# Chunk stage of a delta-rule mixer: two products of 128 columns with one stationary tile, and PSUM banks laid out anew

## What is computed

```python
def rwkv7_recurrence(r, decay, k, v, a, b):
    def step(state, inp):
        r_t, w_t, k_t, v_t, a_t, b_t = inp
        sa = jnp.einsum('bhij,bhj->bhi', state, a_t)
        state = (state * w_t[:, :, None, :]
                 + sa[..., None] * b_t[:, :, None, :]
                 + v_t[..., None] * k_t[:, :, None, :])
        y_t = jnp.einsum('bhij,bhj->bhi', state, r_t)
        return state, y_t
```

## Time and profile before

| | us |
|---|---|
| median of 3 runs | 2779.71 |
| lowest and highest | 2776.44, 2783.08 |
| profiled execution, its own time | 2776.74 |
| span of its trace | 2774.9 |
| TensorE busy in the span | 2632.4 |

### The profile page before, as it was taken

One profiled execution on the slowest core, in us unless ns is written; L12 is line 12 of the kernel. 1 busy time (PEld: TensorE's weight loads), 2 busy tenths in 40 slices (PEclk: granted clock), 3 DMA queues, 4 the chain that ended last, 5 costly groups with the idle time before them and its releaser, 6 DMA issues. The chain is left out here.

```text
span 2774.9 us, 55421 instructions
## 1 busy us (share of the span) xinstructions
PE 2632.4 (95%) x23093; PEld 2112.7 (76%) x23093; DVE 1573.4 (57%) x1945; ACT 1187.9 (43%) x1525; POOL 310.9 (11%) x356
## 2 busy tenths in 40 slices
PE   8999999999999988999999998998789999999998
PEld 7677778888777766888888887844678787788887
DVE  6747455244574655667766666467455555554462
ACT  5544343122464443555665554254224343432232
POOL 5022000000111401011111111021310000000002
PEclk9999999999999989999999999999999999999999
DMA  4200244333220022787778875312014252334341
GB/s 138 79 9 3 62 114 108 82 101 100 81 91 9 4 54 105 279 287 277 280 278 287 284 277 184 97 31 65 4 33 131 78 155 63 91 91 114 84 114 52
DMA packets 351896, 331.31 MB, mean 119 GB/s; under 512 B 17274, under 2 KB 269526, under 8 KB 351606
## 3 DMA queue, kind: packets, MB, share of 16 engines
q1 hardware_dynamic: 348101, 317.76, 36.9%
q0 software_dynamic: 3392, 11.14, 1.1%
q10 hardware_dynamic: 240, 0.07, 0.0%
HBM read 317.41 MB, written 11.53 MB: 119 GB/s over the span
## 5 line engine op out<-in xcount | busy, mean ns | idle before, releaser
L3109 DVE TENSOR_TENSOR experts_w_lo<-experts_raw,experts_w_hi 128x2048 fp32r<-128x2048 f32 (+1 forms) x81 | 167.8, 2079 | 77.3 <-ACT experts_w_hi L3065 75.7
L3109 DVE TENSOR_TENSOR experts_w_lo<-raw_in_act,experts_w_hi 128x2048 fp32r<-128x2048 f32 (+1 forms) x81 | 167.0, 2078 | 60.1 <-ACT experts_w_hi L3065 59.7
L3065 ACT ACTIVATE experts_w_hi<-raw_in_act 128x2048 fp32r<-128x2048 f32 (+1 forms) x81 | 139.7, 1745 | 50.8 <-DMA raw_in_act<-in_moe_up 45.2
L3278 PE MATMUL experts_psum<-experts_w_hi,experts_xg_lo 128*128 128x512 f32 x384 | 154.6, 403 | 5.5 <-DVE experts_w_lo L3109 4.3
L1555 PE MATMUL proj_psum<-keep_act_hi,proj_w_lo 128*128 128x512 f32 x360 | 152.2, 423 | 4.4 <-DVE proj_w_lo L1475 4.4
L3279 PE MATMUL experts_psum<-experts_w_lo,experts_xg_hi 128*128 128x512 f32 x384 | 150.4, 392 | 0.0
L3280 PE MATMUL experts_psum<-experts_w_hi,experts_xg_hi 128*128 128x512 f32 x384 | 150.2, 391 | 0.0
L3065 ACT ACTIVATE experts_w_hi<-experts_raw 128x2048 fp32r<-128x2048 f32 (+1 forms) x81 | 140.5, 1742 | 21.6 <-DMA experts_raw<-in_moe_gate 15.5
L1557 PE MATMUL proj_psum<-keep_act_hi,proj_w_hi 128*128 128x512 f32 x360 | 141.9, 394 | 0.0
L1556 PE MATMUL proj_psum<-keep_act_lo,proj_w_hi 128*128 128x512 f32 x360 | 141.5, 393 | 0.0
L831 PE MATMUL conv_ffn_psum<-keep_act_hi,conv_ffn_w_lo 128*128 128x512 f32 x336 | 132.0, 393 | 2.0 <-DVE conv_ffn_hid_lo L880 2.0
(11 more groups left out here) (896 smaller groups left out, 6807.9 us busy)
## 6 DMA issues: line engine op xcount, KB each, us to landing
raw_in_act<-in_moe_gate SPq DMA_DIRECT2D x33, 1024.0 KB, 8.5
experts_raw<-in_moe_up SPq DMA_DIRECT2D x32, 1024.0 KB, 10.5
experts_raw<-in_moe_down SPq DMA_DIRECT2D x32, 768.0 KB, 10.1
raw_in_act<-in_moe_down SPq DMA_DIRECT2D x32, 768.0 KB, 7.0
conv_ffn_raw<-in_w_ffn_in SPq DMA_DIRECT2D x43, 512.0 KB, 5.0
experts_raw<-in_moe_gate SPq DMA_DIRECT2D x17, 1024.0 KB, 9.0
raw_in_act<-in_moe_up SPq DMA_DIRECT2D x16, 1024.0 KB
proj_raw<-in_w_in SPq DMA_DIRECT2D x18, 768.0 KB, 4.4
```

The lines of the kernel that those rows point to most:

```text
L3065: act.activation(w_hi[v % 2][:, s], raw[ring][:, 0:n], ACT.Copy).then_inc(rounded, 1)
L3109: dve.tensor_tensor(w_lo[v % 2][:, s], raw[ring_of(2 * v + q)][:, 0:n], w_hi[v % 2][:, s].bitcast(F32), ALU.subtract).then_inc(split, 1)
L3278: pe.matmul(out, lhs[1][:, first + k, :], w_hi[slot][:, cols], start=begin and k == 0, stop=False)
```

## The change

1. A form takes 128 columns. `k` and `b` stay stationary, and one product now reads `q` and `a` side by side: an access of two rows of features apart (`r.qa_t`), 64 columns from each. Two forms of 16 products take the place of four. To have `q` and `a` at a fixed distance, `rw`, `bonus`, `g` and `kkb` become views of one tensor `all_rows`; `kkb` thereby lives through the two later parts of the mixer, which put `h_hi` and `o` into its place instead of allocating them.
2. The forms of a pair fill banks 0 to 3 wholly, 256 columns for each of the two results. VectorE masks in the order nt, qb, ak, qk.
3. The row halves of `nt` are exchanged by two products of 512 columns instead of 16 of 64, and wait for `z_kept`. Products with `v` are in the order z, y.
4. A result of a pair takes one bank (`one`, `at`) instead of half of two. In the levels, products use banks 0 to 3 in turn, squares banks 4 and 5 (for `x`) and 6 and 7 (for `xt`) in turn, so squares wait for the additions of two steps before instead of one.
5. `tz` takes banks 4 to 7, one a pair, and no longer waits for a copy.

```diff
-            return ps[:, 2 * s:2 * s + 2, 0:TT * CH].rearrange("p k (t n) -> p k t n", t=TT)
+        def raw(b, w):
+            return ps[:, b:b + 2, w * TT * CH:(w + 1) * TT * CH].rearrange("p k (t n) -> p k t n", t=TT)
+        def at_two(b, out, bank, t):
+            return ps[rows(out), b + bank, t * CH:(t + 1) * CH]
+        def one(b):
+            return ps[:, b, :].rearrange("p (k t n) -> p k t n", k=2, t=TT)
+        def at(b, out, k, t):
+            return ps[rows(out), b, (k * TT + t) * CH:(k * TT + t + 1) * CH]
...
-            def form(s, p, lhs, rhs, done):
+            def form(b, p, lhs, done):
                 for k, half, t in by_head:
-                    last = pe.matmul(place(s, half, k, t), lhs[rows(k), p, chunk(t, half)], rhs[rows(k), p, chunk(t, half)],
-                                     start=True, stop=True)
+                    both = ps[rows(half), b + k, :].rearrange("p (w t n) -> p w t n", w=2, t=TT)[:, :, t, :]
+                    last = pe.matmul(both, lhs[rows(k), p, chunk(t, half)], r.qa_t(rows(k), p, chunk(t, half)), start=True, stop=True)
...
             def swap_halves(p):
-                for k, half, t in by_chunk:
-                    last = pe.matmul(place(3, 1 - half, k, t), m.eye[rows(half), :], nt[rows(half), p, k, t, :], start=True, stop=True)
+                pe.wait_ge(z_kept, p + 1)
+                for half in range(2):
+                    last = pe.matmul(ps[rows(1 - half), 5, :], m.eye[rows(half), :], nt[rows(half), p].rearrange("p k t n -> p (k t n)"),
...
                 if p:
                     pe.wait_ge(formed, 4 * p)
-                if p >= 2:
-                    pe.wait_ge(x_new, p - 1)
-                    pe.wait_ge(z_kept, p - 1)
-                    pe.wait_ge(y_kept, p - 1)
-                    pe.wait_ge(nt_swapped, p - 1)
-                form(0, p, r.b_t, r.a_t, raw_n)
-                form(1, p, r.k_t, r.a_t, raw_a)
-                form(2, p, r.b_t, r.q_t, raw_q)
-                form(3, p, r.k_t, r.q_t, raw_k)
+                form(0, p, r.b_t, raw_b)
+                form(2, p, r.k_t, raw_k)
...
             def squares(l, p):
-                pe.wait_ge(p1_kept, from_1(l, p))
+                n = from_1(l, p) - 1
+                pe.wait_ge(p1_kept, n + 1)
                 pe.wait_ge(xt_new, step_of(l - 1, p))
-                if from_1(l, p) > 1:
-                    pe.wait_ge(xt_new, step_of(l, p) - 1)
+                if n >= 2:
+                    pe.wait_ge(xt_new, step_of(l, p) - 2)
                     if l < L - 1:
-                        pe.wait_ge(x_new, step_of(l, p) - 1)
+                        pe.wait_ge(x_new, step_of(l, p) - 2)
...
-            for s, done, dst, mask in ((0, raw_n, nt, m.before), (1, raw_a, ak, m.before), (2, raw_q, r.qb, m.upto),
-                                       (3, raw_k, qk, m.upto)):
+            for b, w, done, dst, mask in ((0, 1, raw_b, nt, m.before), (0, 0, raw_b, r.qb, m.upto), (2, 1, raw_k, ak, m.before),
+                                          (2, 0, raw_k, qk, m.upto)):
...
+                r.qa_t = lambda rows, p, cols: all_rows[rows, p:p + to_keys + 1:to_keys, cols]
```

More of the change, by code:

```diff
@@ L1103, in _ @@
             from_v(pairs - 1)
-            pe.wait_ge(nt_swapped, pairs - 1)
             swap_halves(pairs - 1)
             def products(l, p):
+                n = from_1(l, p) - 1
                 pe.wait_ge(masked, step_of(l, p))
                 pe.wait_ge(x_new, step_of(l - 1, p))
-                if l == 1:
-                    pe.wait_ge(x_new, pairs)
-                    pe.wait_ge(z_kept, pairs)
                 for k, half, t in by_chunk:
-                    last = pe.matmul(place(p % 2, half, k, t), nb[rows(1 - half), p, k, t, :], x[rows(1 - half), p, k, t, :], start=True,
+                    last = pe.matmul(at(n % 4, half, k, t), nb[rows(1 - half), p, k, t, :], x[rows(1 - half), p, k, t, :], start=True,
                                      stop=True)
@@ L1130, in squares @@
                     if l < L - 1:
-                        last_x = pe.matmul(place(2, 1 - half, k, t), xt[rows(half), p, k, t, :], p1[rows(half), p, k, t, :], start=True,
+                        last_x = pe.matmul(at(4 + n % 2, 1 - half, k, t), xt[rows(half), p, k, t, :], p1[rows(half), p, k, t, :], start=True,
                                            stop=True)
-                    last = pe.matmul(place(3, half, k, t), p1[rows(half), p, k, t, :], xt[rows(half), p, k, t, :], start=True, stop=True)
+                    last = pe.matmul(at(6 + n % 2, half, k, t), p1[rows(half), p, k, t, :], xt[rows(half), p, k, t, :], start=True, stop=True)
                 if l < L - 1:
@@ L1149, in _ @@
                 for k, half, t in by_half:
-                    last = pe.matmul(place(p % 2, k, half, t), r.a_tok[rows(half), t, cols(p, k)], xt[rows(half), p, k, t, :],
+                    last = pe.matmul(at_two(2 * (p % 2), k, half, t), r.a_tok[rows(half), t, cols(p, k)], xt[rows(half), p, k, t, :],
                                      start=True, stop=True)
                 last.then_inc(w_full, 1)
-                if p == 1:
+                if p == 2:
                     pe.wait_ge(xt_new, L * pairs)
-                if p >= 2:
-                    pe.wait_ge(tz_kept, p - 1)
                 pe.wait_ge(z_kept, p + 1)
                 for k, half, t in by_chunk:
-                    last = pe.matmul(place(2 + p % 2, half, k, t), xt[rows(half), p, k, t, :], z[rows(half), p, k, t, :],
+                    last = pe.matmul(at(4 + p, half, k, t), xt[rows(half), p, k, t, :], z[rows(half), p, k, t, :],
                                      start=True, stop=True)
@@ L1191, in first_level @@
                 dve.wait_ge(y_full, p + 1)
-                dve.tensor_tensor(x[:, p], eight(m.eye[:, :]), slot(0), ALU.add).then_inc(x_new, 1)
+                dve.tensor_tensor(x[:, p], eight(m.eye[:, :]), one(4), ALU.add).then_inc(x_new, 1)
             for p in range(pairs):
-                for s, done, dst, mask in ((0, raw_n, nt, m.before), (1, raw_a, ak, m.before), (2, raw_q, r.qb, m.upto),
-                                           (3, raw_k, qk, m.upto)):
+                for b, w, done, dst, mask in ((0, 1, raw_b, nt, m.before), (0, 0, raw_b, r.qb, m.upto), (2, 1, raw_k, ak, m.before),
+                                              (2, 0, raw_k, qk, m.upto)):
                     dve.wait_ge(done, p + 1)
-                    dve.tensor_tensor(dst[:, p], slot(s), eight(mask[:, :]), ALU.mult).then_inc(formed, 1)
+                    dve.tensor_tensor(dst[:, p], raw(b, w), eight(mask[:, :]), ALU.mult).then_inc(formed, 1)
                 if p:
@@ L1206, in _ @@
                         dve.wait_ge(x_new, step_of(l - 1, p))
-                        dve.tensor_tensor(x[:, p], x[:, p], slot(2), ALU.add).then_inc(x_new, 1)
+                        dve.tensor_tensor(x[:, p], x[:, p], one(4 + (from_1(l, p) - 1) % 2), ALU.add).then_inc(x_new, 1)
                     dve.wait_ge(xt_full, from_1(l, p))
                     dve.wait_ge(xt_new, step_of(l - 1, p))
-                    dve.tensor_tensor(xt[:, p], xt[:, p], slot(3), ALU.add).then_inc(xt_new, 1)
+                    dve.tensor_tensor(xt[:, p], xt[:, p], one(6 + (from_1(l, p) - 1) % 2), ALU.add).then_inc(xt_new, 1)
             for p in range(pairs):
@@ L1213, in _ @@
                 dve.tensor_copy(r.tz_tok[:, :, p * P:(p + 1) * P].rearrange("p t (k d) -> p k t d", k=2),
-                                slot(2 + p % 2)).then_inc(tz_kept, 1)
+                                one(4 + p)).then_inc(tz_kept, 1)
 def scan_and_read_phase(m, r, then):
@@ L4239, in rows_job, with cross_mixer @@
     return job
-def cross_mixer(m, q, k, mem_hi, mem_lo):
+def cross_mixer(m, q, k, mem_hi, mem_lo, o_at):
     i = m.ins
```

70 lines of the change are left out of this document (35 added, 35 removed).

## The result

The changed kernel takes 2771.54 us (median of 8 runs, 2759.22 to 2778.42), the kernel before 2784.45 beside it (8 runs, 2776.44 to 2793.46). The ratio is 0.9948, 95% interval 0.9928 to 0.9967: by the ratio 14.5 us less, by the two medians 12.9, against 13.2 forecast. The profiled execution spans 2776.6 us, 1.7 more than that of before. The stage itself gave 15.6 us back, so the windows come first: forms, levels 1 to 4, level 5 and the end, and the scan behind them (columns as in the earlier trace rows).

What follows compares the result with a forecast made beforehand. Code fetch for TensorE was taken as the floor, with waits for other engines added where pauses fall between. Savings of 8.2 + 2.9 + 2.1 = 13.2 us from the median of 2779.71 gave 2766.5 us, range 2759 to 2775.

Steps and rivals of the forecast that it cites:

- The bound: Whole stage: TensorE waits for its code, in blocks of some 126 load-and-matmul pairs, 3.75 us each.
- Forms and first level: Forms part: fewer, wider matmuls mean less code, 24.7 us against 32.88, 8.2 us less.
- the turn: Forms part, each pair after the first: forms, first level, z, y, exchange and wait for z, 5.7 us.
- the prediction's best case: Upper bounds of the three parts' gains: 8.9 + 5.3 + 2.9 = 17.1 us less.
- Levels 1 to 4: The squares' wait goes, code stays: 12.5 blocks at 3.75, 46.8 us against 49.73, 2.9 us less.
- Level 5 and the end: Waits for VectorE go: 3.9 blocks of code, 14.8 us against 16.90, 2.1 us less.
- What comes later is again TensorE's, so what is saved stays saved.: After the chunk stage: the stage's whole gain of 13.2 us reaches the kernel's end.
- my fifth rival: After the stage: clock falls elsewhere or a pause gives the gain back; within 5 us of before; 5%.
- Products that don't overlap: Forms and exchange: wide products hold all four quarters, 3.5 us a form, 11.2 us lost, 2791; 4%.
- forms at half rate: Forms: each 64-column piece costs a whole matmul, 1.84 us a form, 5.8 us gain left, 2774; 8%.
- Levels that follow only waits and work: Levels: code isn't the floor, 31.0 us instead of 49.73, 29 us less in all, 2751; 3%.
- Levels at 4.0 us a block: Levels: a block takes 4.0 us, waits or not, so they stay; 9.4 us less in all, 2770; 15%.

Runs made afterwards that it cites:

- padding: The changed kernel with 16 extra one-column products before each product of the levels: 2782.26 us in one run, levels 1 to 4 at 60.9 us.
- the five products: Unused full-array 256-column products, three after the last tz and two at the scan's start: changed kernel 2768.95 us (ratio 0.9923), kernel before 2781.94 us (0.9971).

## Why the prediction was right

**The bound.** Right: blocks of code are the floor. Narrowing the forms brings the pauses back, the pauses for issue are the only ones left to TensorE in the levels, and with padding a block takes the same time though more work is in it. The chain of argument (equal counts between pauses, packets of 16 KB) holds. Level blocks took 3.74 to 3.95 us, the whole of levels 1 to 4 was 45.44 / 12.5 = 3.64 a block. Packets were 22, one more than said.

**Forms and first level**, 24.7 forecast, 23.40 measured. A form at 0.90 instead of 0.92 and the second pair at 3.70 instead of 3.75 were as said. The mis-sized term is the turn: 5.23 us (1954.94 to the next exchange at 1960.17) and not 5.7. It was put together from operations one behind the other, and they overlap on different quarters of the array. First level and `z` took 1.69 us (1952.38 to 1954.07) against 0.98 + 0.94; `y` and the wait 0.87 (to 1954.94) against 0.98; the exchange and the next forms 2.66 (to 1957.60) against 2.79, as two wide products leave two quarters free. Three turns make 1.4 us. The wait itself was sized about right: it had 0.5 us, and moving the exchange out of its way saved 0.45 a turn (1.35 for three). The 0.24 us of idle time understate it, since the last matmul's own 0.22 us before them count as busy. The clock did not fall in the part, as said: 1.00 in the window. The 8.9 us that the prediction's best case gives this part are worked out nowhere in it; the part gained 9.5, and by the second trace of the kernel before 7.7.

**Levels 1 to 4**, 46.8 forecast, 45.44, and 44.3 to 47.1 in other traces: within its bounds of 44.4 and 49.7, but for a tenth. But I credited the gain to the squares' wait alone. With the old wait it is already 47.35, below the 49.73 of before (49.40 in its second trace), so some of it came with the new layout or with where the code is cut; how much is not separated.

**Level 5 and the end**, 14.8 forecast, 15.18 here: 1.7 less and not 2.1, and it was the wait, as said. In another trace of the changed kernel the part is 0.6 longer than here (16.85 less 16.28), so the forecast was a little too good.

**The sum.** In the profiles the stage gained 15.6 us against 13.2; the runs gained 14.5 by the ratio and 12.9 by the medians. The changed kernel's median is 2771.54 and not 2766.5, since the kernel before, forecast from, had 2779.71 in three runs and 2784.45 in eight. That the gain of the medians lies so close to the forecast is partly luck, since each is drawn from two groups of executions 11 us apart. The pair that is free of this, the kernels with the five products, differs by 2781.94 - 2768.95 = 13.0 us (on one chip, but in two groups of runs, so only roughly).

**"What comes later is again TensorE's, so what is saved stays saved."** The profiled execution speaks against it, by 11.2 us in the scan. It was my fifth rival (the clock falls elsewhere) in one execution, but the kernel before seems to do it as often (13 of 20 against 12 of 24 of the changed kernel at 0.973 or less), so it isn't the change's price. Had I looked only at the two spans, 2774.9 and 2776.6, I would have called the change worthless.

**The other rivals.** Products that don't overlap, and forms at half rate: 1.80 us for two forms excludes both. Levels that follow only waits and work, 31.0 us: excluded by 45.44 with no wait left and 11.6 us of pauses for issue. Levels at 4.0 us a block: 3.64.

## What to carry to other kernels

Where TensorE stops for "issue" with its operands ready, count the matmuls between two such stops and the packets of the instruction queue: if both fit, make the code shorter. Fewer and wider matmuls can then gain even where the array streams as many columns. A wait that is removed gains only down to the time of the code: 7.6 us of waits were worth 0.9 to 2.6 here. Before a padding test is read, look up in the trace what the padding costs the engine itself. Before two spans are compared, compare them stage by stage with the granted clock beside them.

## What the runs showed that was not expected

A stage can keep the low clock though TensorE hardly rests in it:

```profile
2036.00:2044.00 8.00, 8.00 (x137) 8.00 (x134) 2.71 (x6) 0.00 (x0) 0.00 (x0) 0.50 0.01 2
```

The matmul rows are busy for all of 8.00 us, with the thin 64x64 matmuls of the scan, and the clock stays at 0.50 for 41.0 us in all, from 2033.9 on: 36 us in the scan and 5 in the stage behind it. The same 576 matmuls at 1.00 are done in 27 us. Five full-array products at the stage's entry, 0.9 us of the scan's time and some more before it, go with 28 executions of four variants of which none is at 0.973 or less. That they do it by the density of work at the entry is the theory on which they were made, and not shown: they also shorten TensorE's idle time right before the scan's first matmul, from 1.07 us to 0.30; that the low clock doesn't rise again in the scan is what both slow traces show, and why is open. A slow scan of the kernel before was never profiled; its share there is inferred from the clocks of its executions and from the run with the five products.
